# Hybrid decoder block on one core: TensorE's FFN loop written out, with other orders of the upper and lower weight halves

## The reference

```python
def conv_ffn(xn, w_up, conv_w, conv_b, w_down):
    h = causal_dwconv(xn @ w_up, conv_w, conv_b)      # w_up: 2048 x 11264
    a, b = jnp.split(h, 2, axis=-1)
    return (jax.nn.silu(a) * b) @ w_down              # w_down: 5632 x 2048
```

## Time and profile before

| what | value |
|---|---|
| median of the runs | 1511.31 us |
| the profiled execution's own time | 1510.21 us |
| its span | 1508.4 us |
| TensorE busy | 1493.1 us, 99% |
| weight loads (PEld) busy | 1280.1 us, 85% |
| VectorE busy | 1076.9 us, 71% |
| ScalarE busy | 818.1 us, 54% |
| DMA engines, mean rate | 192 GB/s |
| granted TensorE clock | 0.999 of full |

### The profile page before, as it was taken

How to read it: one execution, slowest core, us unless ns; L and a number is a source line. 1 busy time by engine, 2 the same in 40 slices (tenths; PEclk the granted TensorE clock), 3 DMA queues, 4 the chain that set the end, 5 groups by cost and what they waited for, 6 DMA issues and landing times.

```text
span 1508.4 us, 24165 instructions
## 1 busy us (share of the span) xinstructions
PE 1493.1 (99%) x7908; PEld 1280.1 (85%) x7908; DVE 1076.9 (71%) x1576; ACT 818.1 (54%) x1184; POOL 2.9 (0%) x9
## 2 busy tenths in 40 slices
PE   8999999999999999999999999999999999999997
PEld 6888888888888888888888888888888888888886
DVE  5756676788887556665568777777777777777876
ACT  5644478745555546544566454454545555454654
POOL 0000000000000000000000000000000000000000
PEclk9999999999999999999999999999999999999999
DMA  8756655665557554445546655655555556555554
GB/s 307 271 193 219 208 177 190 201 201 167 176 167 240 179 187 160 155 149 195 187 164 199 190 194 187 192 185 194 192 185 195 184 190 195 193 183 191 185 194 139
DMA packets 80314, 288.88 MB, mean 192 GB/s; under 512 B 8928, under 2 KB 10464, under 8 KB 79376
## 3 DMA queue, kind: packets, MB, share of 16 engines
q1 hardware_dynamic: 76320, 276.33, 56.0%
q10 hardware_dynamic: 3456, 8.64, 1.7%
q0 software_dynamic: 496, 3.34, 0.6%
HBM read 286.18 MB, written 2.10 MB: 191 GB/s over the span
## 4 chain that ended last, share of the span: by engine, by line
PE 97%; DVE 1%; ACT 1%; DMA 0%; issue 0%; SPq 0%; ACTq 0%; DVEq 0%
PE ps L261 96%; PE ps L318 0%; DMA raw<-in_stream 0%; DVE wlo L877 0%; ACT whi L527 0%; DVE vm L1354 0%; DVE xres L1364 0%; PE ps L390 0%; ACT scr L761 0%; ACT scr L854 0%; DVE sm_ L1223 0%; DVE xres L1327 0%; SPq L217 0%; DVE wlo L931 0%; ACT vm L867 0%
## 5 line engine op out<-in xcount | busy, mean ns | idle before, releaser
L261 PE MATMUL ps<-xT,whi 128*128 128x512 f32 x2304 | 727.5, 397 | 0.2
L877 DVE TENSOR_TENSOR wlo<-raw,whi 128x1024 fp32r<-128x1024 f32 x516 | 623.3, 1222 | 129.5 <-ACT whi L527 120.0
L527 ACT ACTIVATE whi<-raw 128x1024 fp32r<-128x1024 f32 x516 | 531.7, 1050 | 227.5 <-PE ps L261 220.9
L261 PEld LDWEIGHTS ps<-xT,wlo 128*128 128x128 f32 x2304 | 432.8, 188 | 102.1
L261 PE MATMUL ps<-whi,mixT 128*128 128x512 f32 x1472 | 461.1, 391 | 7.2 <-DVE wlo L935 5.8
L261 PE MATMUL ps<-xT,wlo 128*128 128x256 f32 x2304 | 453.0, 278 | 0.0
L261 PEld LDWEIGHTS ps<-xT,whi 128*128 128x128 f32 x2304 | 352.6, 189 | 2.3 <-DVE wlo L877 0.8
L261 PEld LDWEIGHTS ps<-whi,mixT 128*128 128x128 f32 x1472 | 277.3, 188 | 65.6 <-DVE mixT L926 5.8
L261 PE MATMUL ps<-wlo,mixT 128*128 128x512 f32 x736 | 287.2, 390 | 0.0
L542 ACT ACTIVATE hl<-ps 128x256 f32<-128x256 f32 x160 | 61.1, 382 | 236.7 <-PE ps L261 236.6
L895 DVE TENSOR_TENSOR tmp<-ps,hl 128x256 f32<-128x256 f32 x160 | 67.8, 424 | 146.1 <-ACT hl L542 145.8
(11 more groups left out here) (173 smaller groups left out, 637.4 us busy)
## 6 DMA issues: line engine op xcount, KB each, us to landing
raw<-in_stream SPq DMA_DIRECT2D x519, 512.0 KB, 3.4
xres<-in_xin ACTq DMA_DIRECT2D x2, 1024.0 KB, 6.9
scr<-in_xt_in ACTq DMA_DIRECT2D x8, 256.0 KB, 3.6
xres<-in_xin POOLq DMA_DIRECT2D x1, 2048.0 KB, 12.0
out_x<-vm SPq DMA_DIRECT2D x4, 512.0 KB, 3.1
kT<-in_memt_in SPq DMA_DIRECT2D x2, 512.0 KB, 8.7
vbuf<-in_memin ACTq DMA_DIRECT2D x1, 1024.0 KB, 9.4
gel<-in_memin ACTq DMA_DIRECT2D x1, 1024.0 KB, 7.4
```

The costliest lines, as they stand in the source:

```text
L261: return nc.tensor.matmul(o, l, r, start=start, stop=stop, skip_group_check=True)
L527: A(whi[:, 2 * pr + s, :], raw[:, 2 * pr + s, :], ACT.Copy).then_inc(hi_done, 1)
L877: V.tensor_tensor(wlo[:, 2 * pr + s, :], raw[:, 2 * pr + s, :], f32(whi[:, 2 * pr + s, :]), ALU.subtract).then_inc(lo_done, 1)
```

## The change

The nine passes of TensorE's FFN loop are written out in a Python loop, so each is code of its own and every wait compares with a constant. `narrow` gets a pair of orders, one for each of its two panels. The default is the pairs of before (`PAIRS`). `ONES` goes H(0) L(0) H(1) L(1) and so on. `SKEW` is the same with L one block late. `TURN` and the lists that begin with 2, 3 or 4 differ from `ONES` in the first blocks only. In each pass the first narrow product behind the wide ones takes `FIRST[g - 1]`, and the five others and the two that stand ahead of the next pass's wide products take `AFTER[g - 1]`. The two narrow products at the start of the first pass keep the pairs. The number, the operands and the accumulators of the matmuls are the same, and each panel still begins with H(0) and ends with L(7). Nothing is changed for other engines and for stages outside this loop.

```diff
+def runs(*lengths):
+
+    order, k = [], 0
+    for n in lengths:
+        order += [("H", k + i) for i in range(n)] + [("L", k + i) for i in range(n)]
+        k += n
+    assert k == 8
+    return order
+
+
+ONES, PAIRS = runs(*[1] * 8), runs(*[2] * 4)
+TURN = [("H", 0), ("L", 0), ("L", 1), ("H", 1)] + ONES[4:]
+SKEW = [("H", 0)] + [x for k in range(1, 8) for x in (("H", k), ("L", k - 1))] + [("L", 7)]
+
+FIRST = ((ONES, ONES), (runs(2, 1, 1, 1, 1, 1, 1), ONES), (TURN, ONES), (runs(4, 1, 1, 1, 1), ONES), (SKEW, ONES), (SKEW, SKEW),
+         (PAIRS, PAIRS), (PAIRS, PAIRS), (runs(3, 1, 1, 1, 1, 1), ONES))
+AFTER = ((ONES, ONES),) * 5 + ((SKEW, SKEW), (ONES, ONES), (PAIRS, PAIRS), (ONES, ONES))
...
-            def narrow(m, pr, lhs, at={}):
+            def narrow(m, pr, lhs, at={}, orders=(PAIRS, PAIRS)):
...
-                    for k0 in range(0, 8, 2):
-                        for k in (k0, k0 + 1):
-                            kk = 8 * s + k
+                    for half, k in orders[s]:
+                        kk = 8 * s + k
+                        w = slice(k * P, (k + 1) * P)
+                        if half == "H":
                             if kk in at:
                                 at[kk]()
-                            mm(acc, whi[:, 2 * pr + s, k * P:(k + 1) * P], lhs[:, kk].rearrange("p a b -> p (a b)"), kk == 0, False)
-                        for k in (k0, k0 + 1):
-                            kk = 8 * s + k
-                            last = mm(acc[:, :T], wlo[:, 2 * pr + s, k * P:(k + 1) * P], lhs[:, kk, 0, :], False, kk == KT - 1)
+                            last = mm(acc, whi[:, 2 * pr + s, w], lhs[:, kk].rearrange("p a b -> p (a b)"), kk == 0, False)
+                        else:
+                            last = mm(acc[:, :T], wlo[:, 2 * pr + s, w], lhs[:, kk, 0, :], False, kk == KT - 1)
...
-            with pe.Fori(1, NG - 1) as g:
+            up(C_F // 2 + 4, 2)
+            for g in range(1, NG - 1):
                 m = C_F // 2 - 2 + 6 * g
-                up(m, 2)
                 down(m + 1, g)
-                up(m + 3, 6)
+                up(m + 3, 6, FIRST[g - 1], AFTER[g - 1])
+                if g < NG - 2:
+                    up(m + 6, 2, AFTER[g - 1], AFTER[g - 1])
```

More of the change, by code:

```diff
@@ L477, in _, with up @@
                     wide(C_XO // 2 + 4 * half + n // 2, n % 2, mixT, range(4 * kp, 4 * kp + 4), 2 * g, kp == 0, kp == 3, mid)
-            def up(m, n=2 * GF, at={}):
+            def up(m, n=2 * GF, first=(PAIRS, PAIRS), after=(PAIRS, PAIRS)):
                 for j in range(n):
-                    narrow(m + j // 2, j % 2, xT, {} if j else at)
+                    narrow(m + j // 2, j % 2, xT, {}, after if j else first)
             def down(m, g, k0=0, groups=NCG):
```

## The result

The changed kernel takes 1515.03 us (median of 9 runs, 1514.07 to 1516.63), the kernel before 1510.43 us in its 9 runs. The ratio is 1.0028, 95% interval 1.0019 to 1.0038. So it is slower by 0.28%, 4.2 us (4.6 us by the two medians). The forecast of 1512.9 us had the sign and lies in its range, but the size is well over its +1.6 us, and the interval's lower end is just under the 0.2% at which I had drawn the line. The case I had called likeliest, no change, is not what came.

What follows compares the result with a forecast made beforehand. TensorE's matmuls, by the distance between their starts, were taken as the bound. The profiled 1510.21 us + 1.6 for the orders gave 1511.8; with the profile 1.1 us under the median, the forecast was 1512.9 us, range 1507 to 1518.

Steps and rivals of the forecast that it cites:

- The case I had called likeliest, no change: Whole kernel: a median within about 0.2%, 3.0 us, of before counts as no change; chance of same 0.42.
- What bounds it: Whole kernel: TensorE, busy 99% of 1508.4 us at full clock; only the distance between its matmuls' starts can move the time.
- The loop written out at nothing: TensorE's FFN loop: removing the branch and register steps, and fetching straight code instead, counted as costing nothing.
- Rival D: Nine written-out passes: code fetched too late, about 32 packets with one us exposed at each, +32 us, 1543 us; chance 0.03.
- 928 changes of kind at 1.7 ns: FFN loop's narrow products: 928 added switches between H and L matmuls, 1.7 ns each, +1.6 us.
- B: Narrow products: alternation is itself an even beat; at 340 ns a pair -8.2 us, 1503.1 us, half of that 1507.2; chance 0.20.
- A: Narrow products: alternation never settles, each H and L pays in full, 355 ns a pair, +6.4 us, 1517.8 us; chance 0.35.
- my own sign: Profile of the changed kernel: forecast wrong if the ONES passes differ from 66.4 us by more than 0.4 us each.
- C: ONES passes: beat differs by the first panels ahead, a sum most likely within 3 us of before; counted with the forecast, 0.42.

Runs made afterwards that it cites:

- fours: Pass with all narrow products in runs of four (HHHHLLLL), in a written-out loop with another order in each pass: settled 5613 ns a product, 5573 before.
- eights: Pass with all narrow products in runs of eight, in a written-out loop with another order in each pass: settled 5587 ns a product, 5573 before.

## Why the prediction was right or wrong

- **What bounds it: right.** TensorE alone. The long waits are the same ones, each a little longer.
- **The loop written out at nothing: right**, 0.9998 with pairs, with 23 fetches in the stretch. Rival D is dead.
- **The term that was mis-sized: "928 changes of kind at 1.7 ns", +1.6 us.** The orders cost about 4.1 us in the profiled execution (3.9 narrow, 0.2 wide). The idea behind it failed too, not only its number: fours and eights have fewer changes than pairs and cost more. I had taken the surplus of one mixture over two even beats and divided it by what I could count in it. The surplus belonged to the pattern as a whole. The division was off as well: 696.9 less 692 to 693 ns is 4 to 5 ns a group and not 3.5. By the same reasoning the term would have been +1.8 to +2.3 us, about half of what came.
- **The sign was luck.** The forecast had a surcharge on every change of kind, and the runs show none that goes by their number: with the same alternation behind two groups the kernel is faster than before (1509.01 us). That the sum came out slower hangs on how many passes enter it in a way that leads to the slow beat. The time lies in the range because the range reaches from B to A. And the forecast stands on a median of 1511.31 us, 0.9 us over that of the nine runs, so it looks nearer than the term was. By my own sign ("more than 0.4 us each") the forecast failed: a pass in the slow beat takes 67.0 us, 0.6 or 0.7 more than before. The eighth pass took 66.35 us with groups of 0.70, as I had said, and TensorE waited for nobody at a panel.
- **The sign in the rivals' terms.** A foresaw that alternation never settles and takes 355 ns a pair, +6.4 us. It came to 353.3 in the passes 1 to 5 and the ninth, 5.0 ns a pair over before instead of 6.6. But it does settle, into a pattern of three pairs. B foresaw an even beat at 340 to 344 ns. That exists at 346.7, and one pass of the change runs in it. C, "the beat hangs on how the product is entered", was the mechanism, and I had waved it into the forecast as a mean between the two. It was no mean: of the change's nine passes six enter the alternation into the slow beat and one into the fast one. SKEW has a slow beat of its own, 352.5 ns from both entries that were tried, and one pass keeps pairs.
- **What I could have seen.** The earlier trace rows show that one and the same HHLL takes 0.68 us or 0.70 us, and the starts behind them, to the nanosecond, that the LL of before takes 232 and 228 ns by turns. I used the first as a proof of a price per change. Both were signs of a beat with a memory.
- **The Trainium skill** (TensorE: Matmul & The Clock Gate, LDWEIGHTS) puts a load of 128 columns at P / 1.2 ns, 107 ns. As an estimate from that figure, it would fit behind an L of 113 ns with nothing to pay in any order. The runs disagree: with H's load of 112 columns the pair takes 340.0 ns, the least that was seen with an H of 512 and an L of 256 columns, but with 120 and 128 columns it takes 350.6 and 353.3 ns, and with 96 columns 346.7 ns, so no single load time decides it.

## What to carry to other kernels

Where TensorE is the bound and its matmuls differ in length, the distance between starts is a pattern with a memory: read it over a whole period, behind each kind of entry, before pricing an order by its parts. Here four blocks of a different order at the entry of 256 matmuls were worth 0.84 us each time (45.21 against 44.37 us). An entry is only as steady as what stands ahead of it: behind 96 wide matmuls it came out alike in all nine passes, behind the retention's transposes in two heads of three. So do not count groups from the source. Read in the trace, to the nanosecond, how the last group ahead of the alternation ends.

## What the runs showed of the hardware

- 256-column matmuls follow each other every 119 ns, but one between two of 512 columns takes 112 to 120 ns, and steadily 113 or 114 when the load behind it is of 64 or 112 columns.
- H of 512 and L of 256 columns have two stable alternations, 346.7 and 353.3 ns a pair, and each lasted for seven products (224 matmuls) across panel ends.
- Which of the two it is went with the group HHLL just ahead: last L of 111 to 114 ns fast (158 of 158 places), of 118 to 120 ns behind one of 113 or 114 slow (51 of 51).
- Wide matmuls (512 columns each) forget what stood ahead: in the traces of before and after the distances are back at 226 to 227 ns after at most ten, whatever order ran ahead.
- A loop's branch with more than 700 instructions in its body (352 matmuls and their loads), and the fetching of the same work as straight code (23 packets where the loop had 2), were both without cost to TensorE: 66.35 us a pass either way.
